# The last mixer by tiles: context keys, merge, out projection and queries of tile 0 ahead of tile 1's, with the out weights in the expert ring

## The chip, the core and the metric

One core of a Trainium2 chip runs the whole program in a single launch. The metric is device time in microseconds (us). Five engines work in parallel: PE (TensorE, matrix products), DVE (VectorE), ACT (ScalarE), POOL (GpSimd, here only an issuer of gathers) and SP (SyncE, here only an issuer of loads). Each has its own queue of instructions and goes through it in order; they meet at semaphores. Sixteen DMA engines move the data that SP and POOL ask for.

## The reference

A first block (two attention layers) is followed by a second block of two layers that works on 256 tokens x and 256 context tokens c, width 1024, all in float32. What matters here is the second block's last layer on x. Its context takes part only with keys and values:

```
cn = modulate(rms_norm(hc, norm1_g[l]), mod_c[0], mod_c[1])
kc, vc = split(cn @ wl[:, K_OFF:POOL_OFF])            # last layer: only k and v of the context
o = blocked_diff_attn(q, concat(k, kc), concat(v, vc), lam)
attn = rms_norm(o, attn_norm_g) * (1 - lam_init)       # per head of 128
merged = g[0] * attn + g[1] * pool + g[2] * conv
h = h + mod[2] * (merged @ w_out)
xn2 = modulate(rms_norm(h, norm2_g[l]), mod[3], mod[4])
h = h + mod[5] * peer_ffn(xn2, peer_wq, peer_keys, peer_u, peer_v)
```

`peer_ffn` gives each token 8 heads of 16 experts out of 16384. Queries (`xn2 @ w_q`) are scored against 2 x 128 sub-keys per head; the best 16 of the pair sums are the experts. For each, the row of `peer_u` is multiplied with the token (hidden value), passed through GELU, weighted by a softmax of the scores, and the rows of `peer_v` are summed with these weights. That is 2 x 128 gathered rows of u and as many of v for each of two tiles of 128 tokens; one gather brings one row per token (128 x 1024 float32, 0.5 MB).

## The kernel before

Tokens lie on the 128 partitions, so x and the context are two tiles each (t = 0, 1). The runs are numbered 0 (layer 0, context), 1 (layer 0, x), 3 (layer 1, context keys and values) and 2 (layer 1, x). The order on each engine is written by hand; a ledger (`step`, `at`) names each result and turns the name into a semaphore wait.

Weights come in blocks of up to 1 MB through `wring`, four slots. SP issues the list `W` in order, and block i waits until PE has let go of block i - 4. `before` in the SP part hooks other loads (rows of norm weights, broadcast over partitions into four row buffers) ahead of named blocks. Expert rows go through another ring, `ring`, of eight slots of 0.5 MB. POOL issues the list `ITEMS` in order, and item m waits until item m - 8 has been used (`used_wait`). For run 2 the list is: 32 rows u of (tile 0, group 0); then for each of the seven following (tile, group) pairs u and v alternating, v one group behind u; then the last 32 v and the two modulation rows called gate. A group is two heads, 32 experts. VectorE does the u rows (`expert_rows`), which it spreads between its other instructions at a rate called pace (0.35 rows per instruction in this phase, 0 where the order must be kept clear); PE does nearly all v rows as products with a diagonal matrix (`sum_rows`), which ScalarE makes from the weights (`diags`). PE's sums of run 2 stand in its queue behind the whole of `peer_front(2)`.

The stretch in question, in order of time:

1. Gate 0 (`rows_of("g02")`), while VectorE ends the expert sums of run 0's tile 1 (`rows_upto(0, "gate", 1, 0)`), which complete `h_c`, the context stream. Then `norm(("m", 3))` norms both tiles of the context, PE turns (transposes) both, and `qkv(3, "kv")` multiplies keys and values. `rows_of` takes a weight block for both tiles before it goes to the next block; `tile_by_tile` takes all four blocks for tile 0, then for tile 1.
2. The attention of run 2: 16 units, first the 8 heads of tile 0, then those of tile 1. In iteration u PE makes the scores of unit u, turns the probabilities of u - 2 and makes the values of u - 3. VectorE reduces the maximum, and mixes the two softmaxes; ScalarE takes exponentials and copies. At u = 11 VectorE computes tile 0's statistics (`o_stats`: a product and a reduction over 1024), at u = 13 ScalarE its root, at u = 14 VectorE norms it and merges it with the branches (`o_apply`). Tile 1's come after the loop.
3. PE turns tile 0 of the merged result, turns the sub-keys, and multiplies with the out weights, which come through `wring` (`wo2`): tile 0, then tile 1. `mixed_norm` on VectorE adds the result to h and norms it for the experts, tile 0 then tile 1; the square sums and roots are ScalarE's.
4. `peer_front(2)`: for each group, queries (64 products) of tile 0 and tile 1, then the products with the sub-keys, copied by ScalarE. `choose_and_weigh(2)` on VectorE: choose group 0 of tile 0 in two halves (a head each; after the first half POOL may gather 16 rows), then group 1, then the weights of group 0 (`weigh`: GELU, softmax), and so on. The first u row of a tile waits also for a copy of that tile's input into PSUM (`put_row_input`).

## Time and profile before

| | |
|---|---|
| three timed runs | 3563.33, 3571.93, 3581.46 us; median 3571.93 |
| span of the profiled execution | 3567.6 us; the profile shows no time around it |
| busy | PE 2833.4 (79%), VectorE 2231.3 (63%), POOL 1599.6 (45%), ScalarE 604.0 (17%) |
| mean granted clock of TensorE | 0.946 |
| DMA | 1112.98 MB, mean 312 GB/s |

The span is the time from the first to the last instruction of one execution. The page cuts it into 40 slices of 89 us; slices 30 and 31 (about 2586 to 2765 us) hold the stretch in question. A line of a timeline has the start, the time, the engine, the line of the kernel, the instruction with its output and input, the count, and in brackets the idle time of the engine before it with what ended it. A float32 matmul of 128 x 512 shows as two instructions, so a projection of one tile (8 x 2 products) has 32.

### The profile page before, as it was taken

What the parts mean: (1) busy time and instruction counts of PE and PEld (TensorE: products, weight loads), DVE (VectorE), ACT (ScalarE), POOL (GpSimd) and SP (SyncE); (2) the same over time, 40 slices, a digit from 0 to 9 for tenths busy, and PEclk for the clock granted to TensorE, in tenths of its full rate; (3) what the DMA queues carried; (4) which work ended last, traced back from release to release, by engine and by line L of the source; (5) the groups of instructions that cost most, each with busy time, mean ns of one, the idle gap of its engine ahead of it and who ended that gap; (6) DMA issues with size and microseconds to landing.
All of it is one profiled execution on the core that took longest, in us unless ns stands there. A gap on an engine that the chain in (4) does not pass through costs nothing.

```text
span 3567.6 us, 31289 instructions
## 1 busy us (share of the span) xinstructions
PE 2833.4 (79%) x10826; PEld 1533.8 (43%) x10826; DVE 2231.3 (63%) x4424; ACT 604.0 (17%) x1456; POOL 1599.6 (45%) x1556
## 2 busy tenths in 40 slices
PE   5999998878866999837776676799988956667676
PEld 3557586546333565632222222347544812222222
DVE  1421168888678666796666664587646776666644
ACT  1320011223113101101111111110015111111111
POOL 0000014325437554446666666535400266666665
PEclk8999999888988999969999999999999989999999
DMA  7564469889989889989999999799951699999998
GB/s 261 197 217 151 174 220 337 296 296 350 345 305 323 320 318 350 369 304 364 376 374 363 374 365 376 296 341 371 386 194 36 219 362 362 375 363 367 379 370 334
DMA packets 347192, 1112.98 MB, mean 312 GB/s; under 512 B 37155, under 2 KB 48611, under 8 KB 346140
## 3 DMA queue, kind: packets, MB, share of 16 engines
q0 software_dynamic: 223024, 811.71, 60.9%
q1 hardware_dynamic: 124012, 299.27, 23.4%
q8 instruction: 88, 1.44, 0.2%
q14 instruction: 68, 0.56, 0.0%
HBM read 1106.57 MB, written 4.29 MB: 311 GB/s over the span
## 4 chain that ended last, share of the span: by engine, by line
PE 44%; DVE 16%; POOL 14%; DMA 13%; issue 9%; ACT 2%; another core or an unknown queue 2%; SPq 1%; DVEq 0%; ACTq 0%; POOLq 0%
PE PS L599 20%; POOL ring L1256 14%; PE PS L558 12%; DVE ring L1699 5%; DMA ring<-in_peer_v,eidx 5%; DMA ring<-in_peer_u,eidx 5%; PE PS L683 4%; PE PS L995 2%; PE PS L621 2%; DVE acc L1705 1%; PE PS L704 1%; ACT work L1271 1%; DVE small L2150 1%; DVE work L1790 1%
## 5 line engine op out<-in xcount | busy, mean ns | idle before, releaser
L683 PE MATMUL PS<-ring,diag 128*128 128x512 f32 x1984 | 989.7, 624 | 511.9 <-DMA ring<-in_peer_v,eidx 326.7
L1256 POOL DMA_INDIRECT ring<-in_peer_u,eidx x768 | 796.2, 1037 | 1194.6 <-DVE ring L1699 425.3
L1256 POOL DMA_INDIRECT ring<-in_peer_v,eidx x768 | 793.4, 1033 | 610.5 <-DVE acc L1705 204.2
L1699 DVE SCALAR_TENSOR_TENSOR ring<-ring,PS 128x1024 f32<-128x1024 f32 x512 | 620.8, 1217 | 425.4 <-DMA ring<-in_peer_u,eidx 390.6
L683 PEld LDWEIGHTS PS<-ring,diag 128*128 128x128 f32 x1984 | 346.5, 194 | 1143.1 <-issue 932.9
L599 PE MATMUL PS<-wring,xnT 128*128 128x512 f32 x1344 | 584.4, 596 | 2.8 <-ACT work L1271 1.6
L558 PE MATMUL PS<-xnT,wring 128*128 128x128 f32 (+1 forms) x2896 | 488.4, 331 | 21.8 <-issue 16.1
L558 PEld LDWEIGHTS PS<-xnT,wring 128*128 128x128 f32 x2896 | 444.9, 196 | 64.0 <-issue 24.4
L599 PEld LDWEIGHTS PS<-wring,xnT 128*128 128x128 f32 x1344 | 257.0, 192 | 323.6 <-issue 319.6
L1299 ACT ACTIVATE diag<-const,small 128x128 f32<-128x128 f32 x496 | 188.3, 398 | 974.1 <-PE PS L683 458.4
L1271 ACT ACTIVATE work<-PS 128x512 f32<-128x512 f32 (+4 forms) x333 | 180.8, 578 | 940.9 <-PE PS L558 411.3
L1699 DVE SCALAR_TENSOR_TENSOR ring<-ring,xn_peer 128x1024 f32<-128x1024 f32 x256 | 304.5, 1221 | 33.0 <-DMA ring<-in_peer_u,eidx 31.3
L1784 DVE TENSOR_TENSOR work<-work 128x512 f32<-128x512 f32 (+2 forms) x110 | 83.6, 760 | 187.8 <-ACT work L1395 110.7
L1705 DVE SCALAR_TENSOR_TENSOR acc<-ring,held,acc 128x1024 f32<-128x1024 f32 x127 | 163.1, 1284 | 36.9 <-DMA ring<-in_peer_v,eidx 26.4
L599 PE MATMUL PS<-wring,work 128*128 128x512 f32 x384 | 168.1, 599 | 4.7 <-DVE work L1784 2.6
L1705 DVE SCALAR_TENSOR_TENSOR acc<-ring,small,acc 128x1024 f32<-128x1024 f32 x111 | 142.6, 1284 | 27.5 <-DMA ring<-in_peer_v,eidx 17.2
L599 PEld LDWEIGHTS PS<-wring,work 128*128 128x128 f32 x384 | 73.3, 192 | 97.2 <-issue 90.2
L704 PE MATMUL PS<-wring,cT 128*32 128x128 f32 x1536 | 62.3, 323 | 54.6 <-issue 46.3
L1784 DVE TENSOR_TENSOR work<-PS,work 128x512 f32<-128x512 f32 x32 | 22.1, 690 | 128.5 <-PE PS L558 127.5
L558 PE MATMUL PS<-work 128*128 128x128 f32 (+1 forms) x512 | 78.8, 304 | 22.4 <-ACT work L1271 19.4
L995 PE MATMUL PS<-wring,work 128*128 128x512 f32 x192 | 87.3, 614 | 8.3 <-DMA wring<-in_w_out 5.5
L2150 DVE TENSOR_REDUCE small<-PS 128x2 f32<-128x1024 f32 (+1 forms) x48 | 50.1, 1045 | 65.4 <-PE PS L940 64.7
(214 smaller groups left out, 2068.4 us busy)
## 6 DMA issues: line engine op xcount, KB each, us to landing
wring<-in_w_in SPq DMA_DIRECT2D x128, 1024.0 KB
wring<-in_w_mod SPq DMA_DIRECT2D x48, 1024.0 KB
wring<-in_peer_wq SPq DMA_DIRECT2D x24, 1024.0 KB
wring<-in_ab_w_in SPq DMA_DIRECT2D x13, 1024.0 KB
wring<-in_conv_out_w SPq DMA_DIRECT2D x12, 1024.0 KB
wring<-in_w_out SPq DMA_DIRECT2D x12, 1024.0 KB
ring<-in_peer_u,eidx POOLq DMA_INDIRECT x768
ring<-in_peer_v,eidx POOLq DMA_INDIRECT x768
```

The lines of the kernel that those rows point to most:

```text
L558: ins = pe.matmul(o, a, b, start=(i == 0), stop=(i == n - 1))
L599: ins = pe.matmul(PS[:, banks[t, n], :], lhs[:, 2 * q + kk, t * P:(t + 1) * P], w[:, kk, 512 * n:512 * n + 512], start=(q == kk == 0), sto ...
L683: ins = pe.matmul(PS[:, b + c, :], diag[:, state["summed"] % ND, :], ring[:, m % NG, 512 * c:512 * c + 512], start=(k == SUMS[r, t][0]), s ...
L704: pe.matmul(strips[j], cT[:, kk, :], w(kk, j * P, (j + 1) * P), start=(kk == 0), stop=False)
L995: ins = pe.matmul(PS[:, b, :], OT[:, 2 * q + kk, t * P:(t + 1) * P], w[:, kk, 512 * n:512 * n + 512], start=(q == kk == 0), stop=(q == 3 a ...
L1256: pool.indirect_dma_start(ring[:, m % NG, :], None, tables[kind], bass.IndirectOffsetOnAxis(ap=eidx[:, r % 2, t, k:k + 1], axis=0))\
L1271: A(act.activation(dst, src, ACT.Copy), *tag)
L1299: A(act.activation(diag[:, j % ND, :], ident, ACT.Copy, scale=weights_of(r, t)[:, k:k + 1]), "diag", r, t, k)
L1699: v.scalar_tensor_tensor(out=slot, in0=slot, scalar=1.0, in1=row_input(t) if r else xn_peer[:, t, :], op0=ALU.mult, op1=ALU.mult, accum_ou ...
L1705: v.scalar_tensor_tensor(out=own_sum(r), in0=slot, scalar=weights_of(r, t)[:, k:k + 1], in1=own_sum(r), op0=ALU.mult, op1=ALU.add).then_in ...
L1784: D_(v.tensor_tensor(o, a, b, ALU.mult), *tag)
L2150: D_(v.tensor_reduce(nmax[:, u % 2, 0:2], PS[:, b:b + 2, 0:nk], AX_X, ALU.max, negate=True))
```

## The change

Names are those of the code. The change has these parts:

- Context: norm, turn and keys of run 3 go by tiles. ScalarE and VectorE norm tile 0 ahead of the last expert rows of run 0, tile 1 behind them; PE uses `tile_by_tile` for `k3`. Values stay as they were.
- Attention: the statistics of the output norm are taken by ScalarE, a square with a running sum for each unit, in place of a product and a reduction on VectorE for each tile. Tile 0's root moves from u = 13 to u = 11, its merge from u = 14 to u = 12, and its out projection (`out_tile(0)`) goes into PE's queue ahead of iteration u = 16.
- Out weights: no longer in `wring`; SP loads all four blocks into `ring` (`load_last_out`) once the last eight items of the earlier runs are used. POOL's first gather of run 2 waits until tile 1's out projection has read them.
- Front: tile 0's mixed sum, norm, queries of group 0 and sub-keys come ahead of tile 1's merge on VectorE and of tile 1's projection on PE. Tile 1's mixed sum and norm come on VectorE after the choice of group 0. PE makes tile 0's queries of groups 0 and 1, then tile 1's, then groups 2 and 3 by pairs. `mixed_norm` takes `xn_peer` as scratch for run 2 and an argument `only`; the copy of tile 0's input into PSUM no longer waits for tile 1's turn.

```diff
-O_STATS_AT, O_ROOT_AT, O_APPLY_AT = 11, 13, 14
+O_MEAN_AT, O_APPLY_AT, WO_AT = 11, 12, 16
...
-        quarters(f"wo{r}", "w_out", l, 0)
+        if r != 2:
+            quarters(f"wo{r}", "w_out", l, 0)
...
+        OT_2 = [acc[:, :].rearrange("p (k s) -> p k s", k=KD), OT[:, :, P:S]]
...
+                    if first:
+                        first(u)
                     if u < len(units):
...
+                def context_ready(t):
+
+                    input_turned(3, t)
+                    for g in range(2):
+                        pe.wait_ge(*at("read", "xnT", ("m", 3), t, g))
+
...
+                    elif n == "k" and r == 3:
+                        tile_by_tile("k3", CNT, ("k", 3), context_ready)
...
-                    turn_norm(("m", 3))
-                    wait_norm(("m", 3))
...
                 if r == 2:
-                    merged_turned(0)
+                    attention(r, M_UNITS[r], scores, turns, values, None, lambda u: out_tile(0) if u == WO_AT else None)
+                    state["banks"] = list(range(2, 8))
+                    keys_turned()
+                    return
+
+                attention(r, M_UNITS[r], scores, turns, values, modulate if r == 0 else None)
+                rows_of(f"g0{r}", xnT, ("g0", r))
+                branches(r)
+                keys_turned()
+                for t in range(T):
+                    merged_turned(t)
...
+            def out_tile(t):
+
+                pe.wait_ge(*at("merged", 2, t))
+                turn(MERGEDS[2][:, t, :], ("oT", 2, t), KD)
+                for g in range(2):
+                    pe.wait_ge(*at("read", "oT", 2, t, g))
+                pe.wait_ge(wo_landed, 64)
+                banks = [rot(("wo", 2, t, n)) for n in range(2)]
+                for kk in range(KD):
+                    for n, b in enumerate(banks):
+                        ins = pe.matmul(PS[:, b, :], OT_2[t][:, kk, :], ring[:, kk, 512 * n:512 * n + 512], start=(kk == 0), stop=(kk == KD - 1))
+                        if kk == KD - 1:
+                            done(ins, "wo", 2, t, n)
+
             def peer_front(r):
...
+
+                if r == 2:
+                    of = {}
+                    for g in range(2):
+                        of[g] = halves("pq2", 2 * g)
+                        if g == 0:
+                            turned(0)
+                            normed(0)
+                        queries(0, g, of[g][1])
+                        subkeys(0, g)
+                        if g == 0:
+                            out_tile(1)
+                    turned(1)
+                    normed(1)
+                    for g in range(2):
+                        queries(1, g, of[g][1])
+                        release(*of[g][0])
+                        subkeys(1, g)
+                    for g in range(2, GROUPS):
+                        blocks, w = halves("pq2", 2 * g)
+                        queries(0, g, w)
+                        queries(1, g, w)
+                        release(*blocks)
+                        for t in range(T):
+                            subkeys(t, g)
+                    return
...
+            def load_last_out():
+
+                first = ITEMS.index((2, "u", 0, 0))
+                for m in range(first - NG, first):
+                    sp.wait_ge(*used_wait(m))
+                for q in range(4):
+                    v = DR["w_out_2"][1].rearrange("(k p) n -> p k n", p=P)[:, 2 * q:2 * q + 2, :]
+                    sp.dma_start(ring[:, 2 * q:2 * q + 2, :], v).then_inc(wo_landed, 16)
 
...
+                ("pk2", 0): [(load_last_out,), (load_rows, "m2_2", "n2_2", "sc2_2", "sh2_2")],
             }
...
                     pool.wait_ge(*used_wait(m - NG))
+                if (r, kind, t, k) == (2, "u", 0, 0):
+                    pool.wait_ge(*at("product", "wo", 2, T - 1, 1))
...
+                        if (n, r, t) == ("k", 3, 1):
+                            put_turned(("xnT", ("m", 3), 1), KD, CNT, 1)
...
-                    norm(("m", 3), H["c"], [("h_peer", 0, T - 1), ("g2_merged", r)])
+                    tile_norm(("m", 3), H["c"], 0, ("g2_merged", r))
...
+                    put_turned(("xnT", ("m", 3), 0), KD, CNT, 0)
+                    tile_norm(("m", 3), H["c"], 1, ("h_peer", 0, T - 1))
                     heads_in(3, "kv", l)
...
+                        if r == 2:
+                            A(act.activation(E[:, 128 * (n % 8):128 * (n % 8) + 128], bank("O", r, n)[:, 0:P], ACT.Square,
+                                             scale=head_scale[:, n % 4, 0:1], accum_out=gss[:, qt, h:h + 1]))
...
-                    if r == 2 and u == O_ROOT_AT:
+                    if r == 2 and u == O_MEAN_AT:
                         root(grs[:, 0, 0:8], gss[:, 0, 0:8], ("o_meansq", r, 0), "o_rms", r, 0)
+                    if r == 2 and u == WO_AT - 1:
+                        put_turned(("oT", r, 0), KD, OT_2[0], 0)
...
-                    root(grs[:, 1, 0:8], gss[:, 1, 0:8], ("o_meansq", r, 1), "o_rms", r, 1)
-                    put_turned(("oT", r, 0), KD, OT, 0)
...
+                def mixed_sums(t):
+                    act.wait_ge(*at("h_mix", r, t))
+                    A(act.activation(xn_peer[:, t, :], h[:, t, :], ACT.Square, accum_out=ss[:, t:t + 1]), "sumsq", s, t)
+                    settle()
+                    root(rstd[:, t:t + 1], ss[:, t:t + 1], ("meansq", s, t), "rms", s, t)
+
+                if r == 2:
+                    mixed_sums(0)
+                    keys_in(2)
+                    root(grs[:, 1, 0:8], gss[:, 1, 0:8], ("o_meansq", r, 1), "o_rms", r, 1)
+                    put_turned(("xnT", s, 0), KD, xnT, 0)
+                    queries_in(0, 0)
+                    scores_in(0, 0)
+                    put_turned(("oT", r, 1), KD, OT_2[1], 0)
+                    queries_in(0, 1)
+                    scores_in(0, 1)
+                    mixed_sums(1)
+                    put_turned(("xnT", s, 1), KD, xnT, 1)
+                    for g in range(2):
+                        queries_in(1, g)
+                        scores_in(1, g)
+                    for g in range(2, GROUPS):
+                        for t in range(T):
+                            queries_in(t, g)
+                        for t in range(T):
+                            scores_in(t, g)
+                    return
 
...
-                v.wait_ge(*(at("read", "sub", r, T - 1, GROUPS - 1) if t else at("read", "xnT", ("p", r), T - 1, 1)))
+                v.wait_ge(*(at("read", "sub", r, T - 1, GROUPS - 1) if t else at("read", "xnT", ("p", r), 0 if r == 2 else T - 1, 1)))
...
+                    q, rows_at["pace"] = rows_at["pace"], 0.0
+                    gain("n1_3", "sc_3", "sh_3")
+                    tile_mean(("m", 3), 0)
+                    tile_norm(("m", 3), H["c"], 0, "n1_3", "sh_3")
                     rows_upto(0, "gate", 1, 0)
-                    norm(("m", 3), H["c"], "n1_3", [], "sc_3", "sh_3")
+                    tile_mean(("m", 3), 1)
+                    tile_norm(("m", 3), H["c"], 1, "n1_3", "sh_3")
+                    rows_at["pace"] = q
                     v.wait_ge(*row_wait(f"ag_{r}"))
...
-                    if r == 2 and u == O_STATS_AT:
-                        o_stats(r, 0)
+                    if r == 2 and u == O_MEAN_AT:
+                        o_mean(r, 0)
...
-                    o_apply(r, 1)
                     return
...
+            def o_mean(r, t):
 
                 v.wait_ge(*at("read", "O", r, N_HEADS * (t + 1) - 1))
-                mul(E[:, :], OS[r][:, t, :], OS[r][:, t, :])
-                D_(v.tensor_reduce(gss[:, t, 0:8], E[:, :].rearrange("p (h e) -> p h e", h=8), AX_X, ALU.add))
                 ts(gss[:, t, 0:8], gss[:, t, 0:8], 1.0 / P, EPS, ALU.mult, ALU.add, tag=("o_meansq", r, t))
...
-            def mixed_norm(r, free):
+            def mixed_norm(r, free, only=None):
...
                 v.wait_ge(*row_wait(f"m2_{r}"))
-                if r == 2:
-                    v.wait_ge(mod_stored, 128)
...
-                for t in range(T):
+                for t in (range(T) if only is None else [only]):
                     for n in range(2):
                         v.wait_ge(*at("product", "wo", r, t, n))
-                        o, tmp = h[:, t, 512 * n:512 * n + 512], TOK[:, t, 512 * n:512 * n + 512]
+                        o, tmp = h[:, t, 512 * n:512 * n + 512], (xn_peer if r == 2 else TOK)[:, t, 512 * n:512 * n + 512]
...
+                            mixed_norm(2, [], 1)
                     else:
...
-            mixed_norm(2, [("product", "xnT", ("p", 1), T - 1, 1)])
+            v.wait_ge(mod_stored, 128)
+            mixed_norm(2, [("product", "xnT", ("p", 1), T - 1, 1)], 0)
+            o_mean(2, 1)
+            o_apply(2, 1)
             rows_free(2, "gate", 1, 0)
```

## Rows read from the trace of the kernel before

**Rows 1.** The head of the page.

```profile
span 3567.6 us, 31289 instructions
```

**Rows 2.** Busy time by stretch: count in brackets, then granted clock, DMA share and GB/s.

```profile
2744.00:2803.00 59.00, 55.54 (x296) 38.33 (x294) 29.95 (x68) 12.10 (x24) 0.31 (x1) 0.97 0.34 115
...
2810.00:2820.00 10.00, 7.49 (x37) 6.88 (x37) 3.06 (x10) 1.02 (x2) 2.06 (x2) 0.66 0.71 266
...
2823.00:2858.00 35.00, 29.92 (x268) 29.73 (x266) 33.97 (x94) 6.89 (x11) 15.18 (x16) 0.99 0.77 241
...
2881.00:3558.00 677.00, 475.58 (x958) 165.95 (x957) 408.61 (x925) 91.80 (x249) 446.13 (x474) 0.98 0.98 369
```

**Rows 3.** Timeline of POOL: start, us, instruction, idle before it and its releaser.

```profile
2802.69 0.96 POOL L1256 DMA_INDIRECT ring<-in_peer_u,eidx  x1 [206.76 <-DVE work L2280]
...
2823.23 0.94 POOL L1256 DMA_INDIRECT ring<-in_peer_u,eidx  x1 [10.71 <-DVE ring L1699]
...
2868.68 0.93 POOL L1256 DMA_INDIRECT ring<-in_peer_u,eidx  x1 [0.31 <-issue]
...
2880.72 0.94 POOL L1256 DMA_INDIRECT ring<-in_peer_u,eidx  x1 [2.40 <-DVE ring L1699]
```

**Rows 4.** Timeline from gate 0 to the keys of the context, all engines.

```profile
2579.65 31.92 PE L599 MATMUL PS<-wring,xnT 128*128 128x512 f32 x74
...
2586.29 13.78 DVE L1705 SCALAR_TENSOR_TENSOR acc<-ring,held,acc 128x1024 f32<-128x1024 f32 x10
...
2609.49 1.22 DVE L1724 TENSOR_TENSOR h_c<-h_c,acc 128x1024 f32<-128x1024 f32 x1
...
2613.43 1.28 ACT L1304 ACT_TABLE_LOAD   x1 [0.35 <-DVE small L1796]
...
2624.74 57.21 PE L599 MATMUL PS<-wring,work 128*128 128x512 f32 x128 [1.09 <-ACT work L1271]
```

**Rows 5.** Timeline of TensorE, tile 1 of the queries of run 2.

```profile
2296.37 1.04 PE L566 MATMUL PS<-const,work 128*128 128x128 f32 x8
...
2298.20 13.97 PE L621 MATMUL PS<-wring,xnT 128*128 128x512 f32 x32 [0.79 <-ACT xnT L1271]
```

**Rows 6.** Timelines of VectorE and ScalarE in the last attention.

```profile
2716.03 1.22 DVE L2150 TENSOR_REDUCE small<-PS 128x2 f32<-128x1024 f32 x1
...
2718.73 1.23 DVE L1784 TENSOR_TENSOR work<-h_c 128x1024 f32<-128x1024 f32 x1
...
2735.44 1.22 DVE L2150 TENSOR_REDUCE small<-PS 128x2 f32<-128x1024 f32 x1
...
2701.13 0.69 ACT L1579 ACTIVATE work<-PS,small 128x512 f32<-128x512 f32 x1 [0.20 <-DVE small L1794]
...
2702.47 0.37 ACT L1586 ACTIVATE h_c<-PS,small 128x128 f32<-128x128 f32 x1
```

**Rows 7.** Timelines from the out projection to the first choice.

```profile
2748.14 15.67 PE L995 MATMUL PS<-wring,work 128*128 128x512 f32 x32 [1.89 <-ACT work L1271]
...
2765.37 1.06 ACT L1616 ACTIVATE work<-h_x 128x1024 f32<-128x1024 f32 x1
...
2768.91 1.22 DVE L1787 TENSOR_TENSOR xn_peer<-xn_peer,rows 128x1024 f32<-128x1024 f32 x1
...
2781.10 7.38 PE L558 MATMUL PS<-xnT,wring 128*128 128x128 f32 x64 [0.78 <-ACT xnT L1271]
...
2791.06 0.30 DVE L2279 MAX8 work<-work 128x8 f32<-128x128 f32 x1 [5.51 <-ACT work L1271]
```

**Rows 8.** Timelines from group 1's choice to the first weights, VectorE and ScalarE.

```profile
2820.28 0.29 DVE L2279 MAX8 work<-work 128x8 f32<-128x128 f32 x1 [6.91 <-ACT work L1271]
...
2857.25 1.21 DVE L1699 SCALAR_TENSOR_TENSOR ring<-ring,PS 128x1024 f32<-128x1024 f32 x1
...
2874.37 1.22 DVE L1699 SCALAR_TENSOR_TENSOR ring<-ring,PS 128x1024 f32<-128x1024 f32 x1
...
2878.24 1.57 ACT L1299 ACTIVATE diag<-const,small 128x128 f32<-128x128 f32 x5 [1.48 <-DVE small L1784]
```

More of the change, by code:

```diff
@@ L651, in mod1_unit, with attention @@
                 return f
-            def attention(s, units, scores, turns, values, between=None):
+            def attention(s, units, scores, turns, values, between=None, first=None):
                 state["banks"] = [4, 5] if s in SUMS_PER_UNIT else [4, 5, 6, 7]
@@ L960, in modulate @@
                         modulation(l, 1, u // 2)
-                attention(r, M_UNITS[r], scores, turns, values, modulate if r == 0 else None)
                 def merged_turned(t):
@@ L1612, in scores_in, with queries_in @@
                     copy(SC[t][:, 512 * g:512 * g + 512], bank("sub", r, t, g), "read", "sub", r, t, g)
+                def queries_in(t, g):
+                    act.wait_ge(*at("product", "pq", r, t, g))
+                    copy(PQT[(T * g + t) % 4], bank("pq", r, t, g).rearrange("p (a b) -> p a b", a=4), "read", "pq", r, t, g)
+                def mixed_sums(t):
[21 more added lines that the diff above has]
+                            queries_in(t, g)
+                        for t in range(T):
+                            scores_in(t, g)
+                    return
                 for t in range(T):
```

52 lines of the change are left out of this document (21 added, 31 removed).

## The prediction

> **What bounds the kernel now.** The page comes first: one core, a span of 3567.6 us [rows 1]. The three timed runs give a median of 3571.9 (3563.3 to 3581.5); the span is 4.3 below that median and inside their range, and the trace shows no time around it. I make the sum in the trace and take it off the median; half a per cent, 18 us, is about what a measurement of this kernel can tell from no change.
>
> Next the windows over the last mixer and what follows it [rows 2]. From 2881 to 3558 the DMA engines are 98% busy at 369 GB/s, with no other engine full. That is the stream of expert rows, 514 slots of 0.5 MB for run 2. It can't go faster; it can only start earlier. Ahead of it the DMA engines are almost idle (34% from 2744 to 2803), and from 2823 to 2858 they have 77%, because VectorE hands slots back slowly while it chooses. So the question is by how much the chain up to the stream moves.
>
> The timelines of the chain show its links. POOL issues the first row at 2802.7, fills eight slots, and gets its ninth only at 2823.2, behind VectorE [rows 3]. It issues the 33rd row at 2868.7 and is held once more, until 2880.7, for slots of group (0,1), which VectorE uses after the weights of group (0,0) at 2878.2 [rows 3, 8]. From there on DMA alone decides. The time to watch is the moment when the first weights are ready.
>
> **Part 1, context keys by tile.** TensorE ends gate 0 at 2611.6 and starts the keys at 2624.7, 13.1 us later: it waits for the last expert sum (h_c ends at 2610.7), then both tiles are normed [rows 4]. After, tile 0 is normed from 2586.3 on, beside gate 0's matmuls. That puts about 6 us (gain row 1.2, square and root with a table load 3.2, two passes 2.5, less overlap) ahead of VectorE's ten remaining expert rows, so the last sum ends near 2616 or 2617 rather than 2610.7, and tile 1 is normed by about 2623. The keys of tile 0 need 2.4 us behind gate 0 (eight transposes, two copies), run 2614.0 to 2628.0 (32 matmuls in 13.97 [rows 5]), so tile 1's norm has 5 us of cover. Between the tiles lie 1.8 us, a turn of 1.0 and a wait of 0.8 for its copy, as in the queries of run 2 [rows 5]; keys end at 2643.8. Before, keys and values took 57.2, of which about 2 went at the low clock behind the gap; values take 27.5 more. End of values: 2671.2 for 2681.95, **10.7 us**. SP is past this too: the values' four blocks now wait for tile 1 to read the keys' blocks, one each 3.5 us from 2633.2 to 2643.7, with a nearly idle DMA, and the last is first read at 2664. Bounds: 7 (the norm of tile 1 late by its cover and 4 more) and 12.
>
> From here I keep the clock of the trace of before and take the 10.7 off at the end.
>
> **Part 2, attention.** VectorE loses two passes of 1.23 (statistics), 2.5 us [rows 6]. ScalarE gains a 128-wide square per unit, 0.37 as the copy beside it and a read of the sum. It waits 0.2 for VectorE and about as much for TensorE in a unit of 2.7 us [rows 6]; with 0.46 more I make its round 2.8, that is 0.1 for each of 13 units, 1.3 (bounds 0 and 13 x 0.46 = 6). The two table switches at the root of tile 0 now fall beside VectorE's apply (4.2 us), where they formerly cost VectorE a wait of 1.7. The last reduce moves from 2735.4 to about 2732.9.
>
> **Part 3, tile 0's projection inside the attention.** At u = 16 TensorE turns tile 0, needs ScalarE's copies behind the exponentials of unit 15, and starts at 2737.8. The 32 matmuls took 15.7 after a gap and 14.0 without [rows 5, 7]; I take 15.7: end 2753.5 for 2763.8. The out weights lie in the empty ring: 4 MB asked for by SP after the values' blocks, over 80 us before use, on idle DMA: nothing. Behind it on TensorE are queued the last two turns and three value products; ScalarE copies them until about 2758.6 and only then squares tile 0's mixed sum. Before, from that square's start (2765.4) to the end of the second pass (2770.1) were 4.8 us [rows 7], with the root's table loaded already. Now a load of 1.28 [rows 4] lies on the path: normed at 2764.7.
>
> In the trace the load took 1.28 us and the root followed at once [rows 4]. The Trainium skill (ScalarE: Activation LUTs, "What ACT_TABLE_LOAD costs") puts a switch at about 2.7 us, with a drain; by that the gain would be some 1.4 us less, an estimate by that page.
>
> Then turn and copies (2.6 at the low clock), the query product of group 0 (7.4, and 1.5 for the low clock that the idle TensorE comes back with), copy, sub-keys, copy (2.5): VectorE starts to choose at 2778.7, where it was 2791.1 [rows 7]; tile 1's projection used to stand in between. VectorE's merge of tile 1 (4.2) and ScalarE's key copies lie beside these.
>
> **Part 4, tile 1.** The projection of tile 1 is behind the first sub-keys: 2778 + 1 + 1.1 + 14.0, end 2794.3. A new wait stands here: POOL may not overwrite the ring before. The first choice is ready at 2778.7 + 11.6 = 2790.3, so the first row goes 4 us later than it could, at 2794.5 for 2802.7. This costs the sum nothing: VectorE uses no row until it has chosen the second head (2800.4), a row needs about 6 us, and eight slots are there. Behind this VectorE mixes and norms tile 1: four half passes 2.9, row input and one or two paced expert rows 2.4, then 4.8 as above: 2810.8. It chooses group (0,1) from 2811.3; that took 37.0 [rows 8] with row input 1.2, now 35.8; and then come 15 rows, one every 1.14 us (sixteen before, first and last in [rows 8]): 2864.2, and 0.9 for the first GELU steps.
>
> TensorE is later. From 2810.8: turn and copies 2.6; six query products of 7.4 (44.3), 1.7 at the low clock, the sub-key products and copies in their order 6.2, last copy and table load 2.1: exponentials at about 2869.4, 4 us behind VectorE. So TensorE's queue for tile 1 sets the first weights; with 1.8 for what follows, 2871.2 for 2878.2 [rows 8], 7.0 us. The weight blocks for groups 2 and 3 are issued near 2823 and 2831 beside the rows, 4 MB where 2 MB were. In rows 2 a quarter of 35 us is free there (9 us, 3.4 MB), so I charge 0; bounds 0 and 5. Instruction stalls as in 2810 to 2820, where TensorE had 7.5 of 10 us at clock 0.66 [rows 2], may fall on the tile-1 chain: 0 to 5, I take 0.
>
> **Sum.** 10.7 + 7.0 = 17.7, and about 1.3 us since DMA still had work queued at 2880.7: **19 us**, 3548.5 by the span and 3553 by the median.
>
> **Rivals.** *VectorE sets the first weights* (TensorE keeps up, the square in the attention costs nothing): 4 to 6 us more, gain 24, 3548. For it: the overlap in ScalarE's slack; against it: ten more us of idle TensorE ahead of its queue. *Part of the gain is taken back by TensorE* (attention bound by ScalarE with 0.46 per unit, blocks landing late, a stall of 5): 19 - 4.7 - 5 = 9, 3563; for it speaks the row at clock 0.66. *The stream doesn't move*: the rows sooner asked for are lost again in waits; 0, 3572; against it: 98% DMA from 2881. *Slower*: all query products now stand ahead of the first expert sum on TensorE, and those of groups 2 and 3 wait for 4 MB asked for once tile 1 is done. Each us they land after 2832 (group 2) moves the first weights by one. If the gathers starve each pair of blocks to 30 us after its issue, the pairs come 21 and 5 late, all on the chain: 19 - 26 = 7 us slower, 3579. It decides from about 28 us a pair on; a pair at half of 369 GB/s needs 11.
>
> **How the numbers follow.** Forecast 50%, VectorE rival 14%, partial gain 25%, no move 5%, slower 6%. The gain's own range in the forecast is 14 to 23. Bounds: 28 (12 from part 1, no ScalarE cost, VectorE setting) and 5 (7, 6 and 5 together); with the spread of the runs, 9 to each side of their median, the range is 3540 to 3568. Faster by over 0.5%, below 3554: most of the VectorE rival and rather more than half of the forecast's cases with some of the partial ones' luck, 0.52; within 0.5%: 0.42; slower 0.06.
>
> **What would show it.** Gap of TensorE between gate 0 and keys near 3 us for 13.1; values ending about 10 us sooner; reduces in the attention 2.8 apart; first row at about 2784, and POOL then waiting for tile 1's projection rather than the choice; first weights near 2860 with VectorE waiting about 4 us for ScalarE's exponentials; DMA 98% from there. Wrong if: VectorE doesn't wait there, the keys' second tile waits for the norm, or the windows after 2870 fall below 95% DMA.

## The result, and the profile after

Over 20 runs of each, the changed kernel took 3573.61 us (3567.14 to 3583.40) and the kernel before 3566.65 us (3556.22 to 3581.46). The ratio is **1.0023, 95% interval 1.0014 to 1.0032**: about 8 us slower, where 19 us less was forecast. Beside the experiments the kernel before had medians of 3568 to 3579 us, so everything below goes by ratios taken side by side; 0.001 is 3.6 us.

The profiled execution must be read with care. At 3567.35 us it is among the fastest of its kernel, and its span hardly differs from that of before [rows 1]. The page:

```profile
span 3565.5 us, 31327 instructions
PE 2830.3 (79%) x10826; PEld 1533.4 (43%) x10826; DVE 2225.9 (62%) x4422; ACT 609.1 (17%) x1489; POOL 1612.5 (45%) x1556
...
PEclk8999999889988999979999999999999799999999
...
L561 PE MATMUL PS<-xnT,wring 128*128 128x128 f32 (+1 forms) x2896 | 491.7, 332 | 41.1 <-issue 29.0
```

It was ahead before it came to the change. TensorE ended gate 0 at 2604.3 (in the kernel before at 2611.6, 31.92 us after the 2579.65 of [rows 4]). Over all sixteen profiled kernels of this study that point lies between 2604 and 2620, with the same products on TensorE up to there. So I count from the end of gate 0. The first expert weight (the first diagonal on ScalarE) is 266.6 us behind it in the kernel before [rows 8] and **274.0** in the changed one (forecast: 248.9): 7.4 us later, which is the measured loss. From that diagonal to the end of the span both need the same: 689.4 and 687.2 us.

Busy time by stretch in the changed kernel, with the windows that [rows 2] partly have (count in brackets, then granted clock, DMA share, GB/s):

```profile
2744.00:2803.00 59.00, 43.75 (x222) 34.47 (x221) 40.36 (x117) 6.99 (x13) 12.23 (x13) 0.79 0.31 107
2803.00:2823.00 20.00, 14.12 (x122) 13.55 (x120) 19.41 (x59) 2.39 (x4) 8.52 (x10) 0.93 0.93 332
2823.00:2840.00 17.00, 13.43 (x104) 13.46 (x105) 16.76 (x32) 0.60 (x1) 9.76 (x10) 0.78 1.02 384
2840.00:2858.00 18.00, 9.06 (x43) 8.45 (x43) 7.98 (x18) 1.19 (x2) 7.51 (x8) 0.62 0.80 320
2858.00:2881.00 23.00, 18.35 (x149) 17.16 (x148) 4.10 (x17) 6.19 (x13) 0.64 (x1) 0.94 0.00 1
2881.00:2950.00 69.00, 50.67 (x102) 17.96 (x101) 45.76 (x109) 9.93 (x25) 46.73 (x50) 0.97 0.95 353
```

The reader is to see a full DMA in 2803 to 2840 and one that moves nothing from 2858 to 2881, just before the stretch that DMA bounds. The first row was asked for 28 us sooner than in the trace of before (21 us, counted from gate 0), and then everything stood still. The timeline of TensorE shows on what:

```profile
2718.60 13.97 PE L1027 MATMUL PS<-ring,acc 128*128 128x512 f32 x32 [2.16 <-ACT acc L1335]
...
2745.85 10.23 PE L561 MATMUL PS<-xnT,wring 128*128 128x128 f32 x64 [0.73 <-ACT xnT L1335]
...
2773.44 7.31 PE L561 MATMUL PS<-xnT,wring 128*128 128x128 f32 x64
2787.88 2.08 PE L1055 MATMUL PS<-work 128*128 128x128 f32 x8 [7.14 <-issue]
2795.08 1.97 PE L569 MATMUL PS<-const,xn_peer 128*128 128x128 f32 x8 [5.12 <-DVE xn_peer L1892]
2797.79 9.88 PE L561 MATMUL PS<-xnT,wring 128*128 128x128 f32 x64 [0.73 <-ACT xnT L1335]
...
2817.34 1.16 PE L1055 MATMUL PS<-work 128*128 128x128 f32 x8 [0.69 <-ACT work L1335]
2826.57 13.86 PE L561 MATMUL PS<-xnT,wring 128*128 128x128 f32 x106 [8.08 <-issue]
2841.15 0.50 PE L561 MATMUL PS<-xnT,wring 128*128 128x128 f32 x3 [0.72 <-issue]
...
2847.47 0.37 PE L561 MATMUL PS<-xnT,wring 128*128 128x128 f32 x1 [1.03 <-issue]
2848.87 0.37 PE L561 MATMUL PS<-xnT,wring 128*128 128x128 f32 x1 [1.03 <-issue]
2850.97 0.37 PE L561 MATMUL PS<-xnT,wring 128*128 128x128 f32 x1 [1.73 <-issue]
2852.36 2.72 PE L561 MATMUL PS<-xnT,wring 128*128 128x128 f32 x12 [1.03 <-issue]
2854.88 3.26 PE L1055 MATMUL PS<-work 128*128 128x128 f32 x16
```

And ScalarE, VectorE and POOL in their timelines:

```profile
2738.58 1.28 ACT L1368 ACT_TABLE_LOAD   x1 [0.36 <-DVE small L1901]
2739.87 0.20 ACT L1368 ACTIVATE small<-small 128x1 f32<-128x1 f32 x1
...
2787.23 0.60 ACT L1335 ACTIVATE work<-PS 128x512 f32<-128x512 f32 x1 [27.70 <-remote]
...
2874.93 1.28 ACT L1745 ACT_TABLE_LOAD   x1
...
2878.27 1.57 ACT L1363 ACTIVATE diag<-const,small 128x128 f32<-128x128 f32 x5 [1.69 <-DVE small L1883]
...
2758.66 0.30 DVE L2386 MAX8 work<-work 128x8 f32<-128x128 f32 x1 [11.01 <-ACT work L1335]
...
2876.56 0.19 DVE L2470 TENSOR_REDUCE small<-small 128x2 f32<-128x32 f32 x1 [28.45 <-ACT small L1745]
...
2774.37 0.96 POOL L1320 DMA_INDIRECT ring<-in_peer_u,eidx  x1 [179.90 <-DVE small L2386]
...
2848.97 0.94 POOL L1320 DMA_INDIRECT ring<-in_peer_v,eidx  x1 [0.44 <-issue]
2880.36 0.94 POOL L1320 DMA_INDIRECT ring<-in_peer_u,eidx  x1 [30.45 <-DVE ring L1804]
```

Three waits stand on TensorE's query queue, all of them while the rows come:

1. Query product (0,1) ended at 2780.7 by the timeline, and ScalarE took up its copy at 2787.2. ScalarE was not the late one: in the trace the semaphore that TensorE raises for this product rose only at 2787.21, 6.5 us behind the product, and the copy started 0.02 us later. "remote" only says that the profile can't assign this rise to an instruction. As it models the ends of matmuls, it can't tell whether the product was late or only its signal.
2. The blocks of group 2 were missing until 2826.6: 8.1 us. The second block lands in 16 parts. Of these 13 had landed by 2821.5, the last at 2826.48, 0.09 us before TensorE went on.
3. After 106 of 128 matmuls of group 2 came single ones, mostly 1.4 and once 2.1 us apart. The group ended at 2855.0 instead of 2841.0 (128 matmuls take 14.5): 14 us.

VectorE, with all its rows done at 2848, waited 28.45 us for the exponentials behind TensorE's last group, and POOL 30.45 us for a free slot.

### The profile page after: what moved, and what is told of

Its sections match the earlier page's. It is cut to its first block, busy times and chain, and to the rows that moved or that the text cites. A ratio compares the mean times of both kernels' runs of the same rounds, so it can differ in the third digit from the quotient of the medians.

```text
span 3565.5 us, 31327 instructions
## 1 busy us (share of the span) xinstructions
PE 2830.3 (79%) x10826; PEld 1533.4 (43%) x10826; DVE 2225.9 (62%) x4422; ACT 609.1 (17%) x1489; POOL 1612.5 (45%) x1556
## 3 DMA queue, kind: packets, MB, share of 16 engines
q8 instruction: 88, 1.44, 0.2%
## 4 chain that ended last, share of the span: by engine, by line
PE 45%; POOL 15%; DVE 14%; DMA 14%; issue 9%; ACT 3%; another core or an unknown queue 1%; SPq 0%; DVEq 0%; ACTq 0%; POOLq 0%
PE PS L602 19%; POOL ring L1320 15%; PE PS L561 14%; DMA ring<-in_peer_v,eidx 7%; PE PS L688 5%; DMA ring<-in_peer_u,eidx 4%; DVE ring L1804 4%; PE PS L624 2%; PE PS L1009 1%; PE PS L709 1%; DVE acc L1810 1%; ACT work L1335 1%; DVE work L1895 1%; DVE small L2261 1%
## 5 line engine op out<-in xcount | busy, mean ns | idle before, releaser
L1320 POOL DMA_INDIRECT ring<-in_peer_u,eidx x768 | 810.0, 1055 | 1178.8 <-DVE ring L1804 427.1
L602 PE MATMUL PS<-wring,work 128*128 128x512 f32 x320 | 138.5, 593 | 3.6 <-DVE work L1889 2.6
L602 PEld LDWEIGHTS PS<-wring,work 128*128 128x128 f32 x320 | 60.5, 190 | 79.6 <-issue 74.1
L561 PEld LDWEIGHTS PS<-work 128*128 128x128 f32 x512 | 70.0, 212 | 30.4 <-ACT work L1335 25.0
```

Of the source, the lines that this page charges most:

```text
L561: ins = pe.matmul(o, a, b, start=(i == 0), stop=(i == n - 1))
L602: ins = pe.matmul(PS[:, banks[t, n], :], lhs[:, 2 * q + kk, t * P:(t + 1) * P], w[:, kk, 512 * n:512 * n + 512], start=(q == kk == 0), sto ...
L1320: pool.indirect_dma_start(ring[:, m % NG, :], None, tables[kind], bass.IndirectOffsetOnAxis(ap=eidx[:, r % 2, t, k:k + 1], axis=0))\
```

## The experiments

All times of one line were taken side by side with the kernel before. "Front" is from the end of gate 0 to the first diagonal, "stream" from there to the issue of the 100th row of the last mixer, both from the profiled execution; a profile is one execution, good to a few us.

| kernel | ratio to before, 95% interval | in us | front | stream |
|---|---|---|---|---|
| before | 1 | 0 | 266.6 | 84.2 |
| changed | 1.0023 (1.0014 to 1.0032) | +8 | 274.0 | 83.6 |
| e1 rows without weight | 0.9954 (0.9935 to 0.9972) | -16 | 244.3 | 86.3 |
| e2 blocks of group 2 early | 0.9992 (0.9981 to 1.0003) | -3 | 265.1 | 87.1 |
| e3 sums early | 0.9997 (0.9985 to 1.0010) | -1 | 253.1 | 92.9 |
| e4 both | 0.9973 (0.9960 to 0.9985) | -10 | 247.9 | 93.1 |
| e5 e4, group 3 spread | 0.9950 (0.9933 to 0.9967) | -18 | 247.2 | 88.0 |
| e6 at most 3 rows under way | 0.9944 (0.9923 to 0.9965) | -20 | 253.0 | 87.0 |
| e7 before + context keys by tile | 0.9963 (0.9948 to 0.9978) | -13 | 253.4 | 84.7 |
| e8 e5 + e6 | 0.9982 (0.9969 to 0.9995) | -6 | 243.8 | 103.9 |
| e9 e2 + limit for 32 rows | 0.9966 (0.9954 to 0.9978) | -12 | 253.5 | 84.8 |
| e10 before + limit | 1.0020 (1.0003 to 1.0036) | +7 | 264.7 | 93.2 |
| e11 at most 5 rows under way | 1.0016 (1.0005 to 1.0026) | +6 | 271.8 | 86.0 |
| e12 changed, without part 1 | 1.0071 (1.0052 to 1.0089) | +25 | 285.3 | 86.2 |
| e13 e5 + limit for 32 rows | 0.9935 (0.9913 to 0.9957) | -23 | 243.2 | 87.5 |
| e14 limit for 10 rows | 1.0012 (0.9995 to 1.0029) | +4 | 271.0 | 84.4 |

The change in front plus that in stream gives the timed change within 5 us everywhere but in e6 (-11 for -20, interval -27 to -12). The end is set by when the first weights come and by how well the first rows behind them flow.

### e1: take away the rows' bytes

```diff
+ if r == 2 and m < ITEMS.index((2, "u", 0, 0)) + 40:
+     pool.dma_start(ring[:, m % NG, 0:16], DR["x"][0, 0:P, 0:16]).then_inc(g_landed[m % NG], 16)
+     continue
```

> The changed kernel, with one difference: the first 40 expert rows of the last mixer (those that are fetched before the first expert weights) are a plain copy of 16 columns of x instead of a gather of 1024 columns. This leaves out the contents of these rows; everything that waits for them stays. Theory A (the front of tile 1 lost its gain beside the gathers): in the changed kernel TensorE waited 8.1 us for the weight blocks of group 2 and issued single matmuls 1.4 us apart for about 11 us, both while DMA was at 98% or more. Without the gathers' bytes both should go, first weights about 19 us earlier, time about 3573 - 19 = 3554 us (ratio to before 0.996 to 0.997). Rival B (TensorE's own work and its low clock set the first weights, the gathers are beside the point): the waits shift but the first weights stay, 3573 us, ratio 1.002. Rival C (only the blocks were late, the single matmuls have another cause): 8 us, 3565.

```profile
2819.95 14.46 PE L561 MATMUL PS<-xnT,wring 128*128 128x128 f32 x128
...
2836.08 14.46 PE L561 MATMUL PS<-xnT,wring 128*128 128x128 f32 x128
...
2854.66 0.18 DVE L2473 TENSOR_REDUCE small<-small 128x2 f32<-128x32 f32 x1 [3.85 <-ACT small L1748]
```

e1 leaves out the contents of these rows, so only its time is of use. All three waits are gone, both groups go through in 14.46 us, and VectorE waits 3.85 us for the exponentials where the prediction had "about 4". The time is 3555 for 3574 us of before. That is the forecast, but only for a kernel whose rows weigh nothing. One thing more is changed: POOL asks for plain copies (0.54 us each) and not for gathers (0.94 us). So e1 puts the waits down to the fetching of rows, and doesn't separate their bytes from the way in which they are asked for.

### e7 and e12: the two halves of the change

e7 is the kernel before with part 1 alone, e12 the changed kernel with part 1 undone:

```diff
+ turn_norm(("m", 3))
+ wait_norm(("m", 3))
...
- elif n == "k" and r == 3:
-     tile_by_tile("k3", CNT, ("k", 3), context_ready)
```

> The kernel before with the first part of the change alone: the context's norm, turn and keys go tile by tile. Theory A (this part shortens the path by 10.7 us, and the rest of the kernel is as before: VectorE and not TensorE sets the first weights): 3573 - 10 = 3563 us, ratio 0.997 (0.996 to 0.998). Rival E (what is gained ahead of the gathers is taken back by the same waits behind it): ratio 0.999 to 1.001. Rival F (the keys' second tile waits for its norm, 4 us less): 0.998.

> The changed kernel without its first part: the context's norm is made for both tiles and then turned, as before; attention, out projection and queries as changed. The first part alone took 13 us off the kernel before (ratio 0.9963), and the whole change added 8. Theory A (terms add up, the front's parts cost about 21 us): ratio 1.005 (1.003 to 1.008). Rival J (the first part's gain is lost in the changed front whatever it is, since the first weights hang on something fixed there): ratio 1.002 as the whole change.

Part 1 is worth 13 us (interval 8 to 19), as forecast. Without it the rest costs 25 us. In e12's trace the three waits are of another make-up, and now the one ahead of a pair of ScalarE's copies is the worst:

```profile
2811.02 0.60 ACT L1335 ACTIVATE work<-PS 128x512 f32<-128x512 f32 x1 [29.25 <-remote]
...
2876.40 1.09 ACT L1335 ACTIVATE work<-PS 128x512 f32<-128x512 f32 x2 [20.19 <-remote]
```

By the timeline TensorE had made the query product by 2862.7 and the sub-key product behind it by 2863.8, but its semaphore rose for them only at 2876.37 and 2876.47, and ScalarE started at 2876.40. So the late one is TensorE here too, by 12.6 us behind the second product; the first copy above stands behind a rise that came 8.0 us late. The engine caught is TensorE each time. What differs is the place: a signal, a load of weights or a trickle of single matmuls.

In the kernels with the changed front and no limit on rows (changed, e2, e3, e4, e5, e12) the signal of product (0,1) was 6.5 to 8.0 us late, in the first burst of rows.

### e6, e11, e14, e10: rate or depth?

One more wait on POOL. `n` is 3 in e6, e10 and e14, 5 in e11; it holds for 40 rows, in e14 for 10; e10 puts it into the kernel before.

```diff
+ if first + n <= m < first + 40:
+     pool.wait_ge(g_landed[(m - n) % NG], 16 * ((m - n) // NG + 1))
```

> The changed kernel, with one wait more on POOL: each of the first 40 rows of the last mixer is asked for only when the third row before it has landed, so at most 3 of the 8 slots are under way. Theory A1 (the weight blocks and the engines' instructions stood in the DMA queues behind up to 8 rows): with fewer bytes queued ahead, the 8.1 us wait of TensorE for group 2's blocks and its single matmuls 1.4 us apart fall to less than half; first weights 8 to 15 us earlier, ratio to before 0.997 to 1.000. Rival A2 (it is the rate, not the depth: with three rows under way DMA is as full): waits as in the changed kernel, 1.002. Rival A3 (three rows don't fill DMA, the rows themselves come later and set the weights): row 40 is asked for more than 10 us later than in the changed kernel, ratio 1.000 to 1.005.

> The changed kernel with at most 5 rows under way for the first 40 rows (3 in e6, up to 8 in the changed kernel). Theory A1 (blocks and instructions wait behind the rows that are queued ahead of them): between both, block wait of TensorE 5 to 8 us and some single matmuls, ratio 0.996 to 1.000. Rival (a threshold: DMA is saturated with 5 as with 8): 1.002. Rival (any limit does): 0.9945.

> The changed kernel with the limit of 3 rows under way for the first 10 rows only. In the changed kernel ScalarE took up the copy of query product (0,1) 6.5 us after TensorE had ended it, while the first rows were asked for in one burst; in e6 it took it up at once. Theory A (each stretch of unlimited rows costs its own wait, and they add on TensorE's chain): this wait goes, the later ones (blocks 8.1 us, single matmuls about 11 us) stay: first diagonal 136 us behind the turn of the peer keys (142 in the changed kernel, 121 in e6), ratio 1.000 to 1.001. Rival L (one early limit settles the queues for the whole stretch): as e6, 0.995. Rival M (the ScalarE wait isn't on the chain, since blocks come late anyway): 1.002.

> The kernel before with the limit of 3 rows under way for the first 40 rows. Theory A (in the kernel before TensorE ended its queue some 20 us ahead of need, VectorE's rows set the first weights, so a starved TensorE cost nothing): no gain, ratio 1.000 to 1.003, the small loss for rows that come later. Rival I (a limit on rows under way is worth 28 us in any kernel, for another reason, such as the speed of the gathers): ratio 0.993 to 0.996.

Timelines of e6, then of e14:

```profile
2830.47 16.53 PE L561 MATMUL PS<-xnT,wring 128*128 128x128 f32 x128 [4.63 <-issue]
...
2848.68 14.46 PE L561 MATMUL PS<-xnT,wring 128*128 128x128 f32 x128
...
2867.26 0.19 DVE L2473 TENSOR_REDUCE small<-small 128x2 f32<-128x32 f32 x1 [6.40 <-ACT small L1748]
```

```profile
2784.14 0.60 ACT L1338 ACTIVATE work<-PS 128x512 f32<-128x512 f32 x1 [21.25 <-PE PS L561]
...
2825.68 13.82 PE L561 MATMUL PS<-xnT,wring 128*128 128x128 f32 x103 [7.90 <-issue]
...
2848.60 0.37 PE L561 MATMUL PS<-xnT,wring 128*128 128x128 f32 x1 [2.21 <-issue]
```

With three rows under way the block wait falls from 8.1 to 4.6 us, and the single matmuls and the late signal are gone. By the ratios e6 is 28 us faster than the changed kernel, by the traces 18 (21 in the front, less 3 in the stream); the two were not timed side by side. With five, the block wait is 6.7, the late signal (8.0 us) and the single matmuls are back, and hardly anything is gained. This looks like an edge between three and five, but a limit of five is hardly a limit. In the traces without one, POOL asks for a row every 1.25 us at best, a row lands 4 to 8 us later, and I count at most five under way at any ask, though the ring has eight slots. POOL's waits for a landing show it (us in total, times, longest; e6, then e11, from 2775 to 2876):

```profile
POOL ring L1323 <- DMA ring<-in_peer_u,eidx: 24.6, 13, 3.7
POOL ring L1323 <- DMA ring<-in_peer_u,eidx: 1.9, 2, 1.2
```

So e11 is nearly the changed kernel over again, and a limit of four was not tried. With three for the first 10 rows, exactly the first wait goes and the other two stay. The front became 3.0 us shorter by it, where I had put 6. So each burst of rows brings its own wait. In the kernel before the same limit brings nothing and costs 7 us, because there the 41st row is asked for 10.3 us behind the first diagonal (2.5 without it). So the limit is not worth 20 to 30 us as such: it pays only where TensorE's front is late.

### e2 to e5: blocks early, sums early

e2 loads group 2's blocks into words 2048 to 6144 of `work`, which keys and values leave free, when DMA is idle. e3 moves `top_exp(2, 0, 0)` ahead of ScalarE's copies of group 2 and puts group 3's query parts between the first sums:

```diff
+ ("pq2", 3): [(load_third_queries,)],       # SP, e2, e4, e5, e8, e9, e13
...
+ top_exp(2, 0, 0)                           # ScalarE, e3, e4, e5, e8, e13
...
+ for t in range(T):                         # TensorE, the same; the last number is
+     queries(t, 3, w, 1)                    # the sums ahead of each of 8 parts: 1, from e5 on 3
+ sum_rows(2)
```

> The changed kernel, with the two weight blocks of group 2 loaded into the part of the work buffer that keys and values leave free, right after the last value product of the attention (DMA is idle then), so that they don't wait for group 0's blocks to be released nor land beside the gathers. Theory A: the 8.1 us wait of TensorE for them goes; group 3's blocks are asked for some 9 us earlier; the single matmuls 1.4 us apart stay as long as DMA is saturated. First weights 8 us earlier, about 3565 us, ratio to before 1.000 (0.998 to 1.001). Rival (the wait only changes its name: TensorE meets the same instruction trickle earlier, since DMA is saturated from 2810 to 2850 in any case): 0 to 3 us, ratio 1.002. Rival B (TensorE's work alone): the wait goes, 8 us.

> The changed kernel with another order in two queues: ScalarE takes the exponentials of the first choice (0,0) before the copies of groups 2 and 3, and the GELU step and the first diagonals before those of group 3; TensorE makes the 8 query parts of group 3 one by one between the first 8 expert sums, instead of ahead of all. Nothing is added. Theory A (the first weights wait only for TensorE's and ScalarE's queues; VectorE was idle from 2849 to 2876 and DMA from 2855 to 2880): the first weights come about 25 us earlier, and since the stream behind is DMA's at 98% the time falls by about as much less what group 3's products cost in the stream (0 to 8 us): 3549 us, ratio 0.995 (0.993 to 0.998). Rival D (the stream's total sets the end: what is fetched earlier is lost in VectorE's choice of (0,2), which then comes before the rows, or in slots that TensorE frees later): under 5 us from the changed kernel, ratio 1.001 to 1.003.

> Both: group 2's blocks in the free part of the work buffer, and the first exponentials, weights and sums ahead of group 3. Theory A: with the sums early, the first weights are VectorE's (about 2851 in the trace of the changed kernel, when its rows end), and blocks that land 8 us earlier add little, 0 to 5 us: 3546 us, ratio 0.994 (0.992 to 0.997). If the single blocks edit alone gives 8 us and this one adds 8 us to the early sums too, TensorE would still be the last there, against the theory.

> As e4_both, with three expert sums instead of one ahead of each of the 8 query parts of group 3. In e4_both the stream lost 8 us between the 41st and the 60th row (37.3 us after the first diagonal for 28.9 in the changed kernel), while TensorE took 2.0 us of query parts behind each sum and freed slots at the pace at which rows come. Theory A: with two more sums between them TensorE catches up first, and about 6 of the 8 us come back: 3558 us on e4_both's chip, ratio to before 0.9955 (0.994 to 0.997). Rival D (the rows lost are VectorE's, which makes the choice of (0,2) beside its rows): the ratio stays at 0.997.

e2: the block wait went. The late signal of product (0,1) stayed (8.0 us). The single matmuls stayed too, and now fell into group 3: they began 237.6 us behind gate 0, for 236.9 in the changed kernel, so they belong to a moment of the burst and not to an instruction. Front 9 us shorter. e3: front 21 us shorter, of which the stream lost 9 again. My number for e3 (0.995) missed both this loss and a copy that ScalarE started 13.5 us behind its product, since TensorE's signal was 12.5 us late, as in e12. e4 against e3 gained 8 us where I had put 0 to 5. By my own condition TensorE was then still the last in e3, and its late signal, absent in e4's trace, says how. e5 got back 5 of the 9 us of stream: a product between sums must leave TensorE time to catch up.

### e8, e9, e13: the remedies together

> e5_spread and the limit of three rows under way together. If depth is what starves blocks and instructions (A1), some 0 to 5 us under e5_spread, as e5_spread's first weights are VectorE's already: ratio 0.994 to 0.9955. If three rows don't fill DMA (A3), 5 us or more above e5_spread.

> The changed kernel with group 2's blocks in the work buffer (as e2) and at most 3 rows under way for the first 32 rows (as e6, but free from the 33rd on, since in e8 the 40th row was asked for 9 us behind the first diagonal). In e6 TensorE still waited 4.6 us for group 2's blocks and VectorE 6.4 us for the exponentials behind TensorE's last group. Theory A (TensorE's queue alone sets the first weights, and both waits were the rows' doing): they come 4 to 6 us earlier than in e6, first diagonal 116 us behind the turn of the peer keys (121 in e6, 142 in the changed kernel, 133 in e2), ratio 0.993 (0.991 to 0.995). Rival G (the limit on rows and the early blocks take away the same wait): as e6, 0.9945. Rival H (the single matmuls come back, since their cause is not the depth): 133 us, 0.999.

> e8 with its limit of 3 rows under way for the first 32 rows alone (40 in e8, where the 40th row was asked for 9 us behind the first diagonal and the stream began late). Theory A: the 10 us that e8 lost against e5 were this tail of the limit; without it the kernel is e5 again, and since e5's first weights are VectorE's, the limit gives nothing on top: ratio 0.995 (0.993 to 0.997). Rival K (the limit itself slows the rows that VectorE waits for): 0.998 as e8.

In e9, e13 the limit reads `first + 32`. e8's front is among the shortest, but its limit lasted to the 40th row, beyond the first weights, and the stream started 10.5 us late and stayed behind. e13 stops the limit at the 32nd row and is **the fastest of all, 0.9935 (0.9913 to 0.9957)**, 23 us under the kernel before. My expectation that the limit gives nothing on top of e5 missed by 4 us in the front; the timed intervals of e5, e6 and e13 overlap. e9 missed: expected 0.993, measured 0.9966. Its trace has the reason, a signal of TensorE that came 5.4 us late. It fell behind the end of the limit: the 33rd row, the first free one, was asked for at 2844.28, the 40th at 2852.97, with nothing between but POOL's own pace, and TensorE's products ended at 2849.6 and 2850.6 but were signalled at 2856.06 and 2856.16:

```profile
2843.04 0.94 POOL L1338 DMA_INDIRECT ring<-in_peer_u,eidx  x1 [0.52 <-issue]
2844.28 0.94 POOL L1338 DMA_INDIRECT ring<-in_peer_u,eidx  x1 [0.30 <-issue]
...
2852.97 0.93 POOL L1338 DMA_INDIRECT ring<-in_peer_v,eidx  x1 [0.31 <-issue]
...
2856.09 1.09 ACT L1353 ACTIVATE work<-PS 128x512 f32<-128x512 f32 x2 [12.96 <-remote]
...
2856.74 2.07 PE L1058 MATMUL PS<-work 128*128 128x128 f32 x8 [6.10 <-ACT work L1353]
```

So e9 speaks for the limit and not against it: the wait came with the rows that the limit had let go. A kernel that hangs on TensorE's last group stays exposed to such a wait, one whose sums come early doesn't: in e13 TensorE has 17.8 us to spare ahead of its first sum.

```profile
2838.75 2.01 PE L1059 MATMUL PS<-work 128*128 128x128 f32 x16
2858.53 8.20 PE L691 MATMUL PS<-ring,diag 128*128 128x512 f32 x12 [17.78 <-issue]
```

## Why the prediction was wrong

Its steps, from the end of gate 0 (predicted, then measured in the changed kernel):

- **Part 1, keys by tile**: values end at 59.7, 58.8. Right, and e7 confirms the size.
- **Part 2, attention**: last reduce at 110.6, 109.8. Right; a unit takes 2.73 us, the square is hidden.
- **Part 3, tile 0's projection**: ends at 131.2, 128.3 (14.0 us, not 15.7); choice starts at 156.4, 154.4. Right. The table load on the path took 1.28 us and the root followed 0.01 later; the 1.4 us more that the Trainium skill (ScalarE: Activation LUTs, "What ACT_TABLE_LOAD costs") would add for a drain didn't appear.
- **Part 4, POOL's wait**: first row at 172.2, 170.1. Right, and it cost nothing. VectorE through with its rows at 241.9, 243.0. Right.
- **Part 4, TensorE's queue for tile 1**: from the normed tile 1 to the first diagonal 60.4, measured **83.2**. This step failed, in two terms that I set to zero: "I charge 0; bounds 0 and 5" for the blocks, 8.1 measured, and "0 to 5, I take 0" for stalls, 14 measured. A third I had not at all, TensorE's late signal, 6.5 us, which used up the lead of part 3 ahead of tile 1: tile 1's turn began at 190.8 for 188.5 predicted, and at 187.1 in e14, which lacks this wait. With all of them away (e1) the stretch from the normed tile 1 took 58.6 us. The terms that I listed for it add up to 58.7 and not to 60.4: from 2810.8 they lead to 2867.7 for the exponentials, where I wrote 2869.4. So the work was priced right and only the waits were not.

The range doesn't follow from its parts either: the bounds of 28 and 5 us with 9 us of spread to each side give 3535 to 3576, not 3540 to 3568. That does not save the forecast, since its direction was wrong.

The terms of the path were right within 3 us each; the price of contention was wrong by over 20. I reckoned the room in DMA as a mean: a quarter of 35 us free in [rows 2]. But rows don't come evenly [rows 3]. In the changed kernel 30 of them are asked for from 2797 to 2849, 16 MB in 52 us, and with the 4 MB of blocks this is 380 GB/s asked for, no less than the 353 to 370 of the stretches that DMA bounds. It moved 345 GB/s there at a share of 0.94: there was no room. And the waits of engines were in sight in the trace of before, 0.66 of clock and 7.5 of 10 us; they cost nothing there because VectorE set the first weights, and I took them for small [rows 2].

The mechanism that came true is that of the rival "slower", which I gave 6%: all query products stand ahead of the first sum, blocks come late. It had one wait, at a price of 28 us a pair; group 2's pair took 18.9 us from its issue at 2807.7, group 3's was not waited for, and the rest came from the two kinds of wait that it did not name. That its number, 7 us slower, is the one measured is luck.

On how blocks and rows share: from the first record of group 2's blocks to TensorE's start (2809.2 to 2826.6) all blocks together moved 3.1 MB of 6.6, that is 46%, at 381 GB/s; group 3's pair was among them, asked for at 2816.7. The Trainium skill (DMA: Bandwidth & Descriptors, "Queues, rings and completion order") says that each DMA engine goes round its queues packet by packet; with two busy queues of like packets that would be half, an estimate of some 10 us for a pair by that page. The trace agrees as far as the share goes, and 13 of the 16 parts of the second block had landed 13.8 us behind the pair's first issue. The last part came 5.0 us after them, and TensorE waited for that one. From the first issue to the last landing it was 18.8 us here, 17.4 in e11, 15.3 in e6, and 7.9 in e1, whose rows hold 16 columns.

**What stays open** is what holds TensorE's single matmuls and its signals. Shown: they come in bursts of rows, go without the rows' bytes (e1) and with at most three rows under way (e6, and e13 and e9 as long as the limit held). All signals over 2 us late and all trickles of single matmuls ahead of the first weights began with four or five rows under way, in the changed kernel and in e2, e3, e4, e5, e9, e11, e12 and e14. But this number alone is not enough: from 2826.6 to 2840.4 TensorE ran 106 matmuls in 13.86 us beside three to five rows. In the bursts POOL also asks for one gather right behind the other, so no run separates the rows in the DMA queues from POOL's own work on them. Not shown: what TensorE waits for. The supply of instructions is a candidate: they come by DMA too (over the whole run the two queues marked "instruction" moved 88 and 68 packets, 1.44 and 0.56 MB), and the Trainium skill (Runtime: NRT & Kernel Launch, "Instruction fetch mechanics") says that they are fetched in blocks ahead of use and that this is mostly hidden. The traces speak against it: in none of these waits does a packet of these two queues start or end. In the changed kernel those between 2760 and 2860 lie at 2768.6, 2800.4, 2805.4, 2814.5, 2833.4 and 2858.9, took 0.3 to 1.6 us each, and the waits fell into 2780.8 to 2787.2 and 2840.4 to 2852.4.

## What to carry to other kernels

Work moved in front of a burst of transfers is only worth what the engines keep while the burst runs: charge each load, and each long queue of small instructions, that falls beside a burst of large gathers with a wait, and read a stall that costs nothing today as a price that will be due once its engine is last. Put the work that the next stage hangs on first in every queue and limit how many big transfers are under way (three here, for the five that came without a limit), but only until the stage begins that DMA bounds. Compare profiles from a common event ahead of the change, not by their spans.

## What was not expected of the hardware

- Gathers of 0.5 MB, up to five under way, delayed an engine that had all its inputs: TensorE's signals came up to 12.6 us behind the product (e3, e12), and it took 14 us more for 14.5 us of work. At three under way the rate was nearly kept: from the first to the 32nd row 68.5 us in e6 and 64.5 in the changed kernel.
- A weight block waits for the last of its 16 parts: 13 had landed by 2821.5, the last at 2826.48 beside the gathers, where all 16 came within 0.3 us of each other in e1.
- A ring of eight slots never had more than five rows under way, since a row lands 4 to 8 us after its ask and POOL asks for one every 1.25 us. A limit of five therefore changed next to nothing (271.8 us of front, for 274.0 without a limit and 253.0 with three).
